# Expert weights loaded in four parts instead of two, in a two layer mixture of experts

## The reference, cut to what matters

```python
MOE_EXPERTS, MOE_TOP_K, MOE_FF = 32, 2, 512        # D = 1024, S = 256 tokens, float32

def _hier_moe(h, w_group, b_group, w_expert, b_expert, w_gate, w_up, w_down):
    ...                                            # route: two experts per token, weights top_w
    def expert_block(args):
        xb, e = args
        return (jax.nn.silu(xb @ w_gate[e]) * (xb @ w_up[e])) @ w_down[e]
    ...                                            # y = sum over the token's two experts of weight * output
```

## Time and profile before

| | us |
|---|---|
| median of 3 runs | 2279.26 (2278.39 to 2281.38) |
| the profiled execution | 2275.47 |
| its span, first to last instruction | 2273.7 |

### The profile page before, as it was taken

How to read it: one execution, slowest core, us unless ns; L and a number is a source line. 1 busy time by engine, 2 the same in 40 slices (tenths; PEclk the granted TensorE clock), 3 DMA queues, 4 the chain that set the end, 5 groups by cost and what they waited for, 6 DMA issues and landing times.

```text
span 2273.7 us, 30585 instructions
## 1 busy us (share of the span) xinstructions
PE 1951.9 (86%) x9799; PEld 1083.5 (48%) x9800; DVE 782.4 (34%) x1872; ACT 692.3 (30%) x1067; POOL 90.3 (4%) x105
## 2 busy tenths in 40 slices
PE   8899999999899999997876887786896967868884
PEld 4534777645467775554432433333773423323332
DVE  2273333312433334444322332324324323223334
ACT  1142000012400002131543544444002634434553
POOL 2000000000000000000000000000000000000000
PEclk9899999999999999998998998988898988988997
DMA  8674344534934443215899999996545999999993
GB/s 278 230 308 153 126 165 140 205 119 181 394 122 150 155 156 148 117 42 205 322 421 383 361 412 394 413 415 251 214 185 217 387 420 377 412 421 384 409 397 130
DMA packets 84026, 609.19 MB, mean 268 GB/s; under 512 B 16225, under 2 KB 16545, under 8 KB 21745
## 3 DMA queue, kind: packets, MB, share of 16 engines
q1 hardware_dynamic: 72368, 595.03, 66.3%
q0 software_dynamic: 10720, 11.05, 1.4%
q10 hardware_dynamic: 864, 2.19, 0.2%
HBM read 613.45 MB, written 19.92 MB: 279 GB/s over the span
## 4 chain that ended last, share of the span: by engine, by line
PE 67%; DMA 19%; DVE 5%; issue 3%; ACT 3%; DVEq 2%; SPq 1%; ACTq 0%; POOLq 0%
PE ps L835 26%; PE ps L1228 15%; PE ps L1081 13%; DMA big<-in_w_up 8%; PE ps L1093 6%; DMA big<-in_w_gate 5%; DMA big<-in_w_down 4%; PE ps L1230 3%; PE ps L849 3%; ACT big L1703 2%; DVEq L2412 1%; PE ps L1257 1%; DMA c_res<-f_rows,big 1%; DVE hT L2418 1%; PE ps L1220 1%
## 5 line engine op out<-in xcount | busy, mean ns | idle before, releaser
L1228 PE MATMUL ps<-big,hT 128*32 128x512 f32 x3072 | 724.5, 628 | 144.7 <-ACT big L1703 140.6
L1230 PE MATMUL ps<-big,hT 128*32 x1536 | 723.2, 627 | 0.0
L1703 ACT COPY big<-big 128x1024 f32 x384 | 394.8, 1046 | 504.0 <-DVEq L2400 264.7
L2407 DVE TENSOR_SCALAR big<-big 128x1024 f32 x384 | 261.7, 692 | 663.8 <-PE ps L1230 421.8
L1228 PEld LDWEIGHTS ps<-big,hT 128*32 128x32 f32 x3072 | 200.9, 114 | 545.6 <-DVE big L2407 278.0
L1081 PE MATMUL ps<-hT,big 128*128 128x256 f32 x1408 | 311.1, 379 | 0.0
L835 PE MATMUL ps<-big,hT 128*128 128x512 f32 (+4 forms) x792 | 297.8, 534 | 5.6 <-ACT hT L1631 3.4
L1081 PEld LDWEIGHTS ps<-hT,big 128*128 128x128 f32 x1408 | 267.2, 190 | 52.4 <-issue 18.2
L835 PEld LDWEIGHTS ps<-big,hT 128*128 128x128 f32 x792 | 143.1, 193 | 149.6 <-issue 140.2
L835 PE MATMUL ps<-big 64*30 64x256 f32 (+14 forms) x704 | 147.1, 476 | 29.8 <-DVE big L2357 8.3
L1230 PEld LDWEIGHTS ps<-big,hT 128*32 128x32 f32 x1536 | 165.3, 114 | 4.0
(11 more groups left out here) (346 smaller groups left out, 1167.9 us busy)
## 6 DMA issues: line engine op xcount, KB each, us to landing
big<-in_w_down SPq DMA_DIRECT2D x128, 1024.0 KB, 15.9
big<-in_w_gate SPq DMA_DIRECT2D x128, 1024.0 KB, 12.1
big<-in_w_up SPq DMA_DIRECT2D x128, 1024.0 KB, 13.1
big<-in_dense SPq DMA_DIRECT2D x45, 2048.0 KB, 9.3
big<-in_dense SPq DMA_DIRECT2D x52, 1536.0 KB, 6.5
big<-in_dense SPq DMA_DIRECT2D x5, 1024.0 KB, 7.8
big<-y_rows SPq DMA_DIRECT2D x4, 1024.0 KB, 5.8
f_rows<-big ACTq DMA_DIRECT2D x4, 512.0 KB, 8.9
```

Source lines behind the costliest of these rows:

```text
L1228: nc.tensor.matmul(ps[g * SLOTS:(g + 1) * SLOTS, bank, :], xT[:, k, g * SLOTS:(g + 1) * SLOTS], side[:, g - 1, quarter % 2, at:at + BW], s ...
L1230: return nc.tensor.matmul(ps[0:SLOTS, bank, :], xT[:, k, 0:SLOTS], experts3[:, bass.ds(here, 1), kind * CH + row:kind * CH + row + BW] .re ...
L1703: nc.scalar.copy(side[:, 1, quarter % 2, :], experts3[:, bass.ds(there, 1), lo:lo + QW] .rearrange("p a n -> p (a n)")).then_inc(s["side2_ ...
L2407: ts(side[:, 0, quarter % 2, :], experts3[:, bass.ds(there, 1), lo:lo + QW].rearrange("p a n -> p (a n)"), 1.0, None, mult).then_inc(s["si ...
```

## The change

A kind is loaded in four parts of 4 KB per partition (0.5 MB) instead of two of 8 KB. Every part has a semaphore of its own: `slot_full` for part 0 and `part_full[0..2]` for the others. SP issues a part when its one quarter is done in the last round that uses it, and `need_i` holds 12 r + 1 instead of 12 r + 2 accordingly. VectorE waits for the landing of each quarter ahead of each copy and raises `part_landed` twelve times a round instead of six; ScalarE waits for it ahead of each of its copies. The order of the kinds in SP's queue and the order of work in all others stay.

```diff
-        tail_full = [ctx.enter_context(nc.semaphore(f"tail_full{i}")) for i in range(9)]
+        part_full = [[ctx.enter_context(nc.semaphore(f"part{j}_full{i}")) for i in range(9)] for j in range(1, 4)]
...
-                def put(kind, e, q, half):
-                    lo = half * (CH // 2)
-                    full = slot_full if half == 0 else tail_full
-                    sp.dma_start(experts3[:, q, kind * CH + lo:kind * CH + lo + CH // 2],
-                                 weights[kind][bass.ds(e + layer * E, 1), :, lo:lo + CH // 2]
+                def put(kind, e, q, part):
+                    lo = part * QW
+                    full = slot_full if part == 0 else part_full[part - 1]
+                    sp.dma_start(experts3[:, q, kind * CH + lo:kind * CH + lo + QW],
+                                 weights[kind][bass.ds(e + layer * E, 1), :, lo:lo + QW]
                                  .rearrange("a p n -> p (a n)")).then_inc(full[BPE * q + kind], 16)
 
                 def again(e, q, kinds):
-                    quarters = sp.value_load(need_i[0:1, bass.ds(e - BPE, 1)], min_val=2, max_val=12 * ROUNDS)
+                    quarters = sp.value_load(need_i[0:1, bass.ds(e - BPE, 1)], min_val=1, max_val=12 * ROUNDS)
                     for kind in kinds:
-                        for half in range(2):
-                            sp.wait_ge(done.sem, quarters + (done.base + 4 * kind + 2 * half))
-                            put(kind, e, q, half)
+                        for part in range(4):
+                            sp.wait_ge(done.sem, quarters + (done.base + 4 * kind + part))
+                            put(kind, e, q, part)
...
                 if layer == 0:
                     for q in range(3 * BPE):
-                        sp.sem_inc(tail_full[q], 16)
+                        for j in range(3):
+                            sp.sem_inc(part_full[j][q], 16)
...
                 def copy(b, there, j):
                     kind, quarter = j // 4, j % 4
-                    if quarter % 2 == 0:
-                        act.wait_ge(s["half_landed"].sem, s["half_landed"].at(6 * b + 2 * kind + quarter // 2 + 1))
+                    act.wait_ge(s["part_landed"].sem, s["part_landed"].at(12 * b + j + 1))
...
-                L(ts(need_i[:, 0:E - 1], need_i[:, 0:E - 1], 12.0, 2.0, mult, add))
+                L(ts(need_i[:, 0:E - 1], need_i[:, 0:E - 1], 12.0, 1.0, mult, add))
...
-                def tail_landed(kind, loads):
+                def part_landed(kind, loads, part):
 
                     for q in range(BPE):
                         per_layer = 16 * len(range(q, E, BPE))
-                        v.wait_ge(tail_full[BPE * q + kind], loads[q] + (16 + (16 if q == 0 else 0) + per_layer * layer))
+                        v.wait_ge(part_full[part - 1][BPE * q + kind], loads[q] + (16 + (16 if q == 0 else 0) + per_layer * layer))
...
                     if quarter == 0:
                         landed(kind, loads)
-                        v.sem_inc(s["half_landed"].sem, 1)
-                    elif quarter == 2:
-                        tail_landed(kind, loads)
-                        v.sem_inc(s["half_landed"].sem, 1)
+                    else:
+                        part_landed(kind, loads, quarter)
+                    v.sem_inc(s["part_landed"].sem, 1)
```

More of the change, by code:

```diff
@@ L256, in two_blocks @@
             "up_ready", "up_copied", "conv_step", "conv_a", "conv_b", "silu_done", "gated", "aux_loaded",
-            "rows_gathered", "xT_ready", "xT_done", "side1_copied", "side2_copied", "half_landed", "quarter_done",
+            "rows_gathered", "xT_ready", "xT_done", "side1_copied", "side2_copied", "part_landed", "quarter_done",
             "gate_silu", "hidden_done", "hT_ready", "hT_done", "y_ready", "y_stored",
@@ L578, in expert_stages @@
                 rows_gathered=16 * nb, xT_ready=2 * nb, xT_done=2 * nb, side1_copied=12 * nb, side2_copied=12 * nb,
-                half_landed=6 * nb, quarter_done=12 * nb,
+                part_landed=12 * nb, quarter_done=12 * nb,
                 gate_silu=nb, hidden_done=nb, hT_ready=2 * nb, hT_done=2 * nb, y_ready=nb, y_stored=16 * nb)
@@ L780, in load_experts @@
                     sp.wait_ge(chunk_used, n + 1)
-                    put(kind, q, q, 0)
-                    put(kind, q, q, 1)
+                    for part in range(4):
+                        put(kind, q, q, part)
                 after(sp, room)
@@ L785, in load_experts @@
                 for kind in range(3):
-                    put(kind, 2, 2, 0)
-                    put(kind, 2, 2, 1)
+                    for part in range(4):
+                        put(kind, 2, 2, part)
                 after(sp, "route" + tag)
```

## The result

The changed kernel takes 2299.78 us (median, 2298.36 to 2306.49), the kernel before 2278.82 us on the same chip: ratio 1.0101 [1.0086, 1.0116] over four runs of each, which is 23 us [20, 26] of 2278.8 (the medians themselves lie 21.0 apart). It is slower. The forecast was 2295 us, 2272 to 2312. The profiled execution took 2298.36 us (span 2296.3, before 2273.7).

A forecast was written before the change was run, and what follows sets the result against it. Prediction took DMA transfers, not compute, to bound most of the two expert layers, even in dips. Packets +26.9 us less quarters' gain 10.0 gave +16.9, so 2295 us, range 2272 to 2312.

The forecast's parts named there:

- the rival of recovered dips: Expert layers: earlier quarters fill dips that wait for a release, 20 of 34 us recovered, making it faster; chance 0.12.
- Size of a packet: Expert weight loads: 4 KB instead of 8 KB packets take 3.4% more time per byte, costing 26.9 us (bounds 9 and 33).
- The y_rows stretch: 2251 to 2255, fetching y_rows in nearly all 4 KB packets: 407 GB/s, taken as the rate for the change's loads.
- Release and landing by quarters: Expert loads: earlier release and landing of quarters gain 10.0 us in sum.
- the starts and the restart: First reload of either layer and the restart inside 1293 to 1306: earlier release gains 1.3 us each, 3.9.
- the last waits: Last wait of each layer: the first quarter of a landing is copied 1.3 us earlier, 2.6 us gained.
- the dips: Small dips of the mean share in both layers: a tenth of 34 us given back, 3.5 (bounds 0 and 34).
- The reading that was to show the first one: First reload in the first expert layer: 1090 to 1105 was to move more than 297 GB/s.
- A fixed time per DMA: Expert loads: the skill's 2.0 us per DMA alone would add 696 us over 348 loads; forecast held that it overlaps.
- the 5 us of issues: SP's queue: twelve issues per expert take some 5 us, hidden where an expert's bytes take 15; cost 0.
- the second thought: SP's queue: with a limit by number, half the bytes are outstanding, about 5 MB or 12 us, still no empty queue.
- VectorE's and ScalarE's queues: Added waits and signals hide in VectorE's waiting for TensorE, and ScalarE's copy 9 is in time by 1.2 us; cost 0.

The follow-up runs named there:

- e6: Kernel before with weights laid out so one 1 MB DMA per half reads 4 KB rows, nothing else changed: ratio 1.0104 [1.0080, 1.0128], 2298.96 us.
- e1: The change's four 4 KB loads per kind, but released and looked at by halves as in the kernel before: 2306.13 us, ratio 1.0114 to before.
- e5: Kernel before with each half cut into two 0.5 MB DMAs of 8 KB rows, even and odd partitions: 2280.73 us, ratio 1.0017.
- e3: Loads of the kernel before with the change's waits and signals in VectorE's and ScalarE's queues: 2279.18 us, ratio 1.0003 to before.
- e10: Kernel before with only down loaded as one 2 MB DMA of 16 KB rows, released at its last quarter: 2318.57 us, ratio 1.0167.
- e2: Kernel before with each half cut into two 0.5 MB DMAs of 8 KB rows to 64 neighbouring partitions: 2954.5 us, ratio 1.2966.

## Why the prediction was right, and where it was not

**What bounds the kernel.** Right: it was read as bound by the DMA engines in the expert layers even where their mean share dips. e6 leaves all but the packets alone and loses 24 us. Against the rival of recovered dips, which wanted 20 us back: they cost 50 us before and 44 after.

**Size of a packet.** Nearly right, with one term off. The rate is 409 GB/s, not 407, so 348 x 2.49 x (421/409 - 1) = 25.4 us in place of 29.9, less 2 to 3 where the queue was ahead (three rounds of 24.87 us hold 30 loads of 2.49 us, and not the 35 counted). That gives 22 to 23 for a forecast 26.9; e6 measures 22.0 by the layers and 24 by the ratio, e1 24.2 and 26. The y_rows stretch stood for the right size of row, and its whole course was the better guide than its best part (416).

**Release and landing by quarters.** The step that failed is its size: 10.0 us were forecast, and the change lies 3 (ratios) to 6.9 us (layers) under e1, with none at all not excluded. The windows agree: 479 x (1 - 389/409) + 480 x (1 - 388/409) = 48 us of dips in e1,

```profile
1092.00:1571.00 479.00, 374.66 (x2364) 165.61 (x2361) 142.38 (x227) 222.42 (x244) 31.95 (x29) 0.92 1.00 389
1777.00:2257.00 480.00, 374.65 (x2365) 165.12 (x2361) 142.60 (x227) 222.15 (x243) 31.59 (x29) 0.91 1.00 388
```

44 in the change: 4 us. But e6, released by halves too, has 477 x (1 - 390/409) + 479.5 x (1 - 389/409) = 46 by its windows, so 2 of the 4 are noise or go with the number of DMAs. Which of the three terms (3.9 for the starts and the restart, 2.6 for the last waits, 3.5 for the dips) was too large is not settled. The reading that was to show the first one missed: 1090 to 1105 had 297 GB/s, and the stretch that answers to it, 1095 to 1110, has 261.

**A fixed time per DMA.** The Trainium skill ("DMA: Bandwidth & Descriptors", section "Rules for kernel authors") wants at least 1 MiB per DMA. e5 has 0.5 MB in each and moves 421 GB/s as before, e6 has 1 MB in each and moves 409. Here the row decided and not the DMA, and of the 696 us that a fixed time per DMA would be, e5 shows 4 [1, 7]. The fit from which the forecast had the 696 stands in the Trainium skill ("DMA: Bandwidth & Descriptors", section "Anatomy of one DMA — SWDGE (gpsimd) path") and is of DMAs that GpSimd issues; these are SP's.

**SP.** No cost, as forecast, but the 5 us of issues were wrong: in a full queue SP is held for 1.2 us an issue, 14.8 us for an expert. What held was the second thought, that even with fewer bytes outstanding the queue does not run empty (the share stays 1.03). The room between SP and the transfers is used up, and what SP would do next is late by that; here it does nothing else.

**VectorE's and ScalarE's queues.** Right: 0 by e3, and the round of 24.66 us.

**The sum.** +16.9 forecast, +17.3 in the layers, +20 to +26 by the ratio. Cost and gain were both too large, the cost by 3 to 5 us and the gain by 3 to 7, or by all 10 if the quarters bring nothing. The sum came out nearer than its terms because two errors of opposite sign met, and that is luck; the mechanism, a price per packet that outweighs what the grain returns, is what e6 and e1 show. The median is 4.8 us above 2295, about what the ratio and the layers differ by. The time per layer, +7 to 9 forecast, is +7.3 and +10.0, the second above it. Waits for in_w_* grew in sum, more and on the mean shorter (3.1 against 4.6 us), as said; the longest of each did not get shorter (gate's 19.5 against 17.0). The share in saturated windows went to 1.03, not 1.01.

## What to carry to other kernels

Before cutting a load finer, price the row length first: in a bound stream, 8 to 4 KB per partition cost 3% of the rate, whatever the number of DMAs, and a stretch of the same row length elsewhere in the trace tells it beforehand. Grain has falling returns here: from wholes to halves some 60 us, from halves to quarters 3 to 7 or nothing, so ask what the next cut can still release that the last one did not, and which wait it moves: by e10's rows down's is dear because the product stands behind it in VectorE's queue. A dip in the engines' mean share does not say how much can be won: of 60 us in one layer halves won back 34, and of the 50 left in both layers quarters won back at most 6.

## What the hardware showed that was not expected

- **64 neighbouring partitions:** a full queue of 0.5 MB DMAs to partitions 0 to 63 and 64 to 127 in turn moves 235 GB/s (e2); to even and odd partitions, 421 (e5). The DMAs of all the other kernels, e5's too, reach over all 128. The Trainium skill ("DMA: Bandwidth & Descriptors", section "Rules for kernel authors") says that transfers to disjoint partition halves bring nothing as they share the same engines; here they cost 44% of the rate.
- **Rates by row:** 428 to 430 GB/s at 16 KB, 421 at 8, 409 at 4, the last two with 1 or 0.5 MB per DMA alike. 16 x 4096 B / 409 = 160 ns per packet and 311 at 8 KB: 9 ns go with the packet by these two, where 8 and 16 KB gave 13.
- **How much the queue takes:** in 1820 to 1880 a load lands 25 to 26 us after its issue before, 22 in e5, 19 to 20 in e6, 15.5 in the change (median). A load of 4 KB rows in 0.5 MB waits least. SP's rows for in_w_up (issue min/median/max ns) show who is held: before, after, e6.

```profile
L759 SPq DMA_DIRECT2D big<-in_w_up x128: 327/333/2009, 935.3 to 2209.9; - x128
```

```profile
L759 SPq DMA_DIRECT2D big<-in_w_up x256: 14/344/3492, 940.6 to 2233.1; - x128
```

```profile
L759 SPq DMA_DIRECT2D big<-in_w_up x128: 367/373/5859, 935.6 to 2232.2; - x128
```

e6 has the DMAs of before and is held up to 5.9 us by one, against 2.0. So it is not the number of DMAs or bytes outstanding that holds SP: e6 has 7.5 DMAs of 1 MB under way (19.3 us at 2.56 each), before has 10. A limit on packets for each engine would fit, by an estimate from the landing times: 7.5 DMAs of 17 packets in e6, 15.5/1.28 = 12 of 9 in the change (8 rows of 4 KB for each 0.5 MB and one small packet), so some 110 to 130. No run was made to find the limit.
